# The sample group's slots in the attention of a hybrid decoder step: key products earlier, value products further apart, two cache buffers exchanged

## The reference

```python
DIL_CONFIGS = ((128, 1), (512, 4), (2048, 16))
kc = jnp.concatenate([win_k, k], axis=1)      # sample group: cached rows, then the new ones
vc = jnp.concatenate([win_v, v], axis=1)
for _, dil in DIL_CONFIGS:
    o_i, l_i = dilated_branch_sample(q, kc, vc, dil)
...
attn = combine_branches(outs, lses).reshape(B, T, ATTN_WIDTH)
```

## Time and profile before

| what | value |
|---|---|
| median of 3 runs | 1748.76 us (1748.57 to 1753.09) |
| profiled execution | 1746.06 us, span 1744.3 us |
| TensorE matmul busy | 1688.0 us, 97% |
| VectorE, ScalarE busy | 1112.6 us (64%), 914.3 us (52%) |
| stage of the change | about 345 to 524 us |

### The profile page before, as it was taken

The page is one execution under the profiler, slowest core; times in us unless marked ns, Lnnn a source line. Parts: engine busy times, 40 slices in busy tenths (PEclk is TensorE's granted clock), DMA queues, the critical chain, the costliest instruction groups (busy, mean ns, idle before and its releaser), DMA issues.

```text
span 1744.3 us, 29781 instructions
## 1 busy us (share of the span) xinstructions
PE 1688.0 (97%) x11750; PEld 1576.6 (90%) x11750; DVE 1112.6 (64%) x2055; ACT 914.3 (52%) x1673; POOL 2.2 (0%) x12
## 2 busy tenths in 40 slices
PE   7999999989999999999998999999999999999998
PEld 7999999845669999888778999999999999999998
DVE  5489998777665776435457767644676534676533
ACT  7534434755666675545455555444545433555433
POOL 0000000000000000000000000000000000000000
PEclk9999999999999999999999999999999999999999
DMA  9899967495215645443533444444445444445443
GB/s 284 197 248 217 239 169 164 157 323 223 86 56 166 187 139 164 146 133 110 177 95 104 122 121 137 138 133 142 135 138 157 139 136 144 135 134 154 139 138 100
DMA packets 400672, 271.44 MB, mean 156 GB/s; under 512 B 54251, under 2 KB 374881, under 8 KB 399183
## 3 DMA queue, kind: packets, MB, share of 16 engines
q1 hardware_dynamic: 395688, 260.72, 51.9%
q10 hardware_dynamic: 4847, 8.83, 1.5%
HBM read 225.40 MB, written 27.23 MB: 145 GB/s over the span
## 4 chain that ended last, share of the span: by engine, by line
PE 79%; DVE 7%; ACT 5%; DMA 4%; issue 3%; SPq 1%; ACTq 1%; DVEq 0%
PE bank L1344 74%; PE bank L1341 5%; DMA raw<-in_w_in_dram 1%; ACT whi L702 1%; ACT WORDS L823 1%; DVE C L1957 1%; DMA raw<-in_w_mv_dram 1%; DVE wlo L1970 1%; ACT wide L716 1%; DVE cv L1957 1%; DVE Pp L1961 1%; DMA cached<-in_cache_win_v_dram 0%; DVE Y L1957 0%; DMA cached_t<-keys_turned 0%; DVE RSCF L2093 0%
## 5 line engine op out<-in xcount | busy, mean ns | idle before, releaser
L1344 PE MATMUL bank<-op_hi,whi 128*128 128x352 f32 x1632 | 538.8, 330 | 5.1 <-DVE wlo L1970 2.9
L1970 DVE TENSOR_TENSOR wlo<-raw,whi 128x1024 fp32r<-128x1024 f32 (+1 forms) x312 | 374.3, 1201 | 261.0 <-ACT whi L702 260.4
L1344 PE MATMUL bank<-op_hi,wlo 128*128 128x352 f32 x1632 | 524.6, 321 | 0.0
L1344 PE MATMUL bank<-op_lo,whi 128*128 128x352 f32 x1632 | 523.8, 321 | 0.0
L702 ACT ACTIVATE whi<-raw 128x1024 fp32r<-128x1024 f32 (+1 forms) x312 | 325.2, 1043 | 318.8 <-DMA raw<-in_w_down_dram 95.6
L1344 PEld LDWEIGHTS bank<-op_hi,whi 128*128 128x128 f32 x1632 | 306.9, 188 | 14.8 <-issue 10.1
L1344 PEld LDWEIGHTS bank<-op_lo,whi 128*128 128x128 f32 x1632 | 307.9, 189 | 0.6
L1344 PEld LDWEIGHTS bank<-op_hi,wlo 128*128 128x128 f32 x1632 | 306.6, 188 | 0.0
L1344 PE MATMUL bank<-fhi,whi 128*128 128x352 f32 x528 | 171.2, 324 | 0.0
L1344 PE MATMUL bank<-fhi,wlo 128*128 128x352 f32 x528 | 170.7, 323 | 0.0
L1344 PE MATMUL bank<-h1hi,whi 128*128 128x352 f32 x480 | 159.9, 333 | 3.4 <-DVE wlo L1970 3.4
(11 more groups left out here) (290 smaller groups left out, 2274.7 us busy)
## 6 DMA issues: line engine op xcount, KB each, us to landing
raw<-in_w_up_dram SPq DMA_DIRECT2D x132, 512.0 KB, 3.8
raw<-in_w_down_dram SPq DMA_DIRECT2D x48, 512.0 KB, 4.1
raw<-in_w_out_dram SPq DMA_DIRECT2D x24, 512.0 KB, 4.3
raw<-in_w_xq_dram SPq DMA_DIRECT2D x24, 512.0 KB, 4.2
raw<-in_w_xo_dram SPq DMA_DIRECT2D x24, 512.0 KB, 4.2
PLANES<-HALVES SPq DMA_DIRECT2D x96, 112.0 KB, 3.7
keys_turned<-WORDS SPq DMA_DIRECT2D x24, 448.0 KB, 3.2
cached_t<-keys_turned SPq DMA_DIRECT2D x6, 1792.0 KB, 9.5
```

The costliest lines, as they stand in the source:

```text
L1344: return pe.matmul(out, lhsT, rhs, start=first, stop=last, skip_group_check=shared)
L1970: dve.tensor_tensor(wlo[v % SLOTS][:, 0:nk, :], raw[v % SLOTS][:, 0:nk, :], whi[v % SLOTS][:, 0:nk, :].bitcast(F32), ALU.subtract).then_in ...
```

## The change

`PLACES` exchanges the first two buffers: `cached[0]` now lies at 160064, and `cached[1]` at 47104. The queue loads window 0 (k0) at the place where it loaded window 1, and window 1 (k1) after `LAST_IN`, where it loaded window 0. The order of all other windows stays.

The slots are now written out by hand. Group 0: key products at 3, 8, 13 and 17, masked maximum 19, exponential 20, scaling 22, turning Ps 23, PTS 24, value products 25, 30, 34 and 38, copy 40, turn and small copies 41. Group 1: batches 4 and 5 at 3 and 7, tiles at 8 to 21, masked maximum 23, exponential 24, scaling 26, turning Ps 27, PTS 28, value products 29, 33, 36 and 39, copy 41, turn 42. `product_bank` follows the tiles: in the steps that hold tiles the product for the prompt uses bank 3.

```diff
--- before.py
+++ after.py
@@ -209,7 +209,7 @@
     stage_f = mn("stage_f", 146656, [P, 3, P])
 
 
-    PLACES = (47104, 160064, 119808)
+    PLACES = (160064, 47104, 119808)
     cached = [mn(f"cached{i}", o, [P, KTILES, AW]) for i, o in enumerate(PLACES)]
     cached_t = [mn(f"cached_t{i}", o, [P, AT, KEYS]) for i, o in enumerate(PLACES)]
     HALVES = [mn(f"HALVES{i}", 160064 + 3584 * i, [P, 2, KEYS], U16) for i in range(2)]
@@ -339,8 +339,11 @@
     STEPS = [(i, hp) for i in range(TT) for hp in range(AT)]
     NP = len(STEPS)
     LAST_P2 = max(s for s in range(NP) if s % 3 == 2)
-    GROUP = 4 * KTILES
     SAMPLE = 44
+    KEYS_DONE = (18, 22)
+    BATCH_AT = {(0, 3): 0, (0, 8): 1, (0, 13): 2, (0, 17): 3, (1, 3): 4, (1, 7): 5}
+    VALUE_AT = {(0, 25): 0, (0, 30): 1, (0, 34): 2, (0, 38): 3, (1, 29): 4, (1, 33): 5, (1, 36): 6, (1, 39): 7}
+    GATHERED_AT = (40, 41)
     ORDER_W = [(kind, b) for g in range(2) for kind in "kv" for b in range(4 * g, 4 * g + 4)]
     EARLY = 14
     EARLY_OUT = 4
@@ -376,7 +379,8 @@
         return n % 3 != 0
 
     def key_tile(g, r):
-        return g * GROUP + r if 0 <= r < GROUP and (g * GROUP + r) // KTILES >= AHEAD else -1
+        n = 8 * KTILES - KEYS_DONE[1] + r
+        return n if g == 1 and FIRST_TURNED <= n < 8 * KTILES else -1
 
     def product_bank(s):
         return 3 if any(key_tile(*sample_slot(s + 3, pos)) >= 0 for pos in range(3)) else 4
@@ -386,10 +390,6 @@
 
     def pieces_until(u):
         return sum(n for v, n in PIECES_AT.items() if v < u)
-
-    def batch_slot(r):
-
-        return r // KTILES if 0 <= r < GROUP and r % KTILES == KTILES - 1 else -1
 
     QTS = [[(0, P), (P, P), (2 * P, (CW if c < CH - 1 else SP0) - 2 * P)] for c in range(CH)]
     SLOT = {("mix", 2): 0, ("mix", 0): 1, ("mix", 1): 0, ("xq", 2): 1, ("xq", 0): 0, ("xq", 1): 1,
@@ -566,7 +566,7 @@
                     sp.wait_ge(*at(f"kept{i}", PIECES - 2 + i))
                 load(wt[:, :], A["prompt_bias"], "tables", "p")
                 load(ws[:, :], A["sample_bias"], "tables", "s")
-                window(1)
+                window(0)
             weight(u)
             if u in GATHER_AT:
                 gather_old(GATHER_AT[u])
@@ -584,7 +584,7 @@
                     load(stage_u[:, i, :], A["state_conv"].rearrange("a b t c -> (a b t) c")[i * 120:(i + 1) * 120, :], "states", ("u", i))
 
         sp.wait_ge(*at("unit", LAST_IN))
-        window(0)
+        window(1)
         sp.wait_ge(*at("csq_used", 2 * CH - 1))
         sp.wait_ge(*at("cn", (CONV_ORDER[CH - 1], CT - 1)))
         window(2)
@@ -903,16 +903,16 @@
                 if n >= FIRST_TURNED + 2:
                     act.wait_ge(*at("ssc", ("tile", n - 2)))
                 act.activation(KTS[n % 2][:, :, :], bank[4 + n % 2][:, :].rearrange("p (k n) -> p k n", k=AT), ACT.Copy).then_inc(*mark("ktsa", n))
-            if r == GROUP + 2:
+            if r == KEYS_DONE[g] + 2:
                 act.wait_ge(*at("smax", g))
                 act.activation(Ps[:, :], Ps[:, :], ACT.Exp, bias=negm[:, 2:3], accum_out=den[:, 2:3]).then_inc(*mark("sexp", g))
-            if r == GROUP + 6:
+            if r == KEYS_DONE[g] + 6:
                 act.wait_ge(*at("sptr", g))
                 if g:
                     act.wait_ge(*at("spv", 3))
                 act.activation(PTS[:, 4:7, :], bank[7][:, 0:384].rearrange("p (a n) -> p a n", n=P), ACT.Copy).then_inc(*mark("spta", (g, 0)))
                 act.activation(PTS[0:NS, KTILES, :], bank[7][0:NS, 384:512], ACT.Copy).then_inc(*mark("spta", (g, 1)))
-            if r == GROUP + 14:
+            if r == GATHERED_AT[g]:
                 act.wait_ge(*at("spv", 4 * g + 3))
                 if g:
                     act.wait_ge(*at("sot", 0))
@@ -1600,13 +1600,13 @@
                 group_scores(g)
             if key_tile(g, r - 1) >= 0:
                 key_scores(key_tile(g, r - 1))
-            elif batch_slot(r) >= 0:
-                batch_scores(4 * g + batch_slot(r))
-            if r == GROUP + 5:
+            elif (g, r) in BATCH_AT:
+                batch_scores(BATCH_AT[g, r])
+            if r == KEYS_DONE[g] + 5:
                 turn_ps(g)
-            if r - GROUP - 7 in (0, 2, 4, 6):
-                window_product(4 * g + (r - GROUP - 7) // 2)
-            if r == GROUP + 15:
+            if (g, r) in VALUE_AT:
+                window_product(VALUE_AT[g, r])
+            if r == GATHERED_AT[g] + 1:
                 take(5, "satt", (g, 3, 1))
                 pe.wait_ge(*at("os", g))
                 for b in range(4):
@@ -2185,8 +2185,8 @@
                 if n >= FIRST_TURNED + 2:
                     dve.wait_ge(*at("ssc", ("tile", n - 2)))
                 dve.tensor_copy(KTS[n % 2][:, :, :], bank[4 + n % 2][:, :].rearrange("p (k n) -> p k n", k=AT)).then_inc(*mark("ktsd", n))
-            if r == GROUP + 1:
-                dve.wait_ge(*at("ssc", 3 if g == 0 else ("tile", 2 * GROUP - 1)))
+            if r == KEYS_DONE[g] + 1:
+                dve.wait_ge(*at("ssc", 3 if g == 0 else ("tile", 8 * KTILES - 1)))
                 if g:
                     dve.wait_ge(*at("sptr", g - 1))
                 pieces_s = ((0, 512, bank[6][:, 0:512], ws[:, 0:512]), (512, KEYS, bank[7][:, 0:KEYS - 512], ws[:, 512:KEYS]),
@@ -2197,17 +2197,17 @@
                     masked_max(Ps[:, k0:k1], src, bias, mx[:, 0, k:k + 1], mx[:, 0, k - 1:k] if k else -3e38).then_inc(*mark("sm", (g, k)))
                 dve.wait_ge(*at("sm", (g, 2)))
                 dve.tensor_scalar(negm[:, 2:3], mx[:, 0, 2:3], -1.0, None, ALU.mult).then_inc(*mark("smax", g))
-            if r == GROUP + 4:
+            if r == KEYS_DONE[g] + 4:
                 dve.wait_ge(*at("sexp", g))
                 dve.reciprocal(rden[:, 2:3], den[:, 2:3]).then_inc(*mark("srd", g))
                 dve.wait_ge(*at("srd", g))
                 dve.tensor_scalar(Ps[:, :], Ps[:, :], rden[:, 2:3], None, ALU.mult).then_inc(*mark("spn", g))
-            if r == GROUP + 6:
+            if r == KEYS_DONE[g] + 6:
                 dve.wait_ge(*at("sptr", g))
                 if g:
                     dve.wait_ge(*at("spv", 3))
                 dve.tensor_copy(PTS[:, 0:4, :], bank[6][:, :].rearrange("p (a n) -> p a n", n=P)).then_inc(*mark("spt", g))
-            if r == GROUP + 15:
+            if r == GATHERED_AT[g] + 1:
                 dve.wait_ge(*at("sot", g))
                 for b in range(4):
                     v = bank[5][:, b * P:(b + 1) * P].rearrange("p (k y) -> p k y", y=32)
```

## The result

The changed kernel took 1756.14 us (median of nine runs, 1750.58 to 1758.99), the kernel before 1748.89 us on the same chip (nine runs, 1743.3 to 1753.09). The ratio, estimated from the runs, is 1.0033 [1.0021, 1.0045] (the brackets are its 95% interval; the quotient of the medians alone would be 1.0041): **slower by 0.33%, some 5.8 us**. That is at the edge of what the prediction called measurable. The sign of the sum was right (+1.8), its size was three times too small: applied to the median that the prediction started from, the ratio gives 1748.76 x 1.0033 = 1754.5 us, at the upper end of its range (1744.5 to 1755); the median as measured, 1756.14, lies 1.1 above that end.

The account below looks back on a forecast made before the run. TensorE, busy 97% of the span, was taken as the bound, with VectorE bounding steps 4 to 11. Terms +2.0 - 2.0 - 0.4 = -0.4, plus 2.2 for the clock, gave +1.8 us: 1750.5 us, range 1744.5 to 1755.

Parts of the forecast that it names:

- Buffers: nothing: Exchanging the places of k0 and k1: the 0.45 us wait for k0 goes, nothing else changes in the queue there.
- Group 0: +2.0 and +2.2 for the clock: Up to step 15: 2.0 us lost without the clock, 2.2 more from a fall to 1.2 GHz behind the gap before Ps.
- TensorE waits 0.9: Step 5, fourth key product: reached at 363.6, k3's load lands at 364.5, so TensorE waits 0.9 us.
- the chain crossing three small steps: Reason given for group 0's 2.0 us loss: the softmax chain crosses three small steps where TensorE has little else to do.
- a good place for them is in steps 4 to 10: Group 0: VectorE bounds steps 4 to 11, so key products are well placed in steps 4 to 10; no size of its own.
- Steps 15 to 19: gain 2.0: Group 1: gaps of 3.4 us behind VectorE get filled with six more tiles, one 1.4 us gap stays; gain 2.0 us.
- Group 1 behind them: gain 0.4: Second masked maximum holds scores 24 by 1.6 us, Ps waits 0.6, product 0.1, against 1.7, 0.5 and 0.5 before; gain 0.4.
- Later steps are TensorE's own limit, and work moved among them is worth nothing: Group 1 behind step 19: TensorE itself sets the pace, so moving work among these steps gains nothing.
- Rival 1: Gap before Ps: the clock does not fall because VectorE is faster than counted; -0.4 us, 1748.4 us; chance 0.27.
- Rival 2: Attention: the waits go and the chain is hidden, all 7.5 us come back, 1741.3 us; chance of over 5.2 us 0.08.
- Rival 3: Group 0: low clock holds until the fourth value product; slower by more than 0.3%, 1757 us; chance 0.12.
- Rival 4: Step 5: k3 lands later still because v0's load runs beside it; +2.5 us more, 1753 us; chance 0.08.

Follow-up runs that it names:

- e1: Changed kernel with all slots of both groups put back, only the buffers changed: 1748.59 us, ratio 0.999 to the kernel before.
- e2: Changed kernel with group 1's slots put back, so only group 0 and the buffers changed: 1756.00 us, ratio 1.0033 to the kernel before.
- e4: Changed kernel with the load of v0 issued only when k3 has landed: 1757.56 us, ratio 1.0038 to the kernel before.
- e5: Changed kernel with turning Ps, PTS copies and each group's first value product one slot later: 1753.83 us, ratio 1.0036 to the kernel before.
- e9: Against e1, only group 0's key products moved to slots 3, 8, 13 and 17: 1755.66 us, ratio 1.0025 to the kernel before.
- e10: Changed kernel with seven extra unused matmuls filling the gap before group 0's turns of Ps: 1756.50 us, ratio 1.0035 to the kernel before.
- e12: Kernel of e7 with group 0's key products at slots 6, 11, 16 and 20: 1747.99 us, ratio 0.9997 to the kernel before.
- e3: Changed kernel with group 0's slots put back, so only group 1 and the buffers changed: 1752.95 us, ratio 1.0008 to the kernel before.
- e6: e3 with group 1's value products back at their old slots: 1750.26 us, ratio 1.0005 to the kernel before.
- e7: e6 with group 1's tiles, masked maximum, softmax and turn of Ps one slot later: 1747.29 us, ratio 0.9988 to the kernel before.
- e8: Changed kernel with group 0's fourth key product and softmax chain three slots later, value products at 28, 32, 35, 38: 1754.62 us, ratio 1.0033 to before.

## Why the prediction was right and wrong

**Buffers: nothing.** Right (e1); k0's product waited for nothing.

**Group 0: +2.0 and +2.2 for the clock.** The mechanism was right: the gap before Ps was forecast at 4.2 us and was 4.46, the clock fell behind it and stayed low for about 6.8 us (twice what 0.53 and 0.79 lack of 1.00, times 5 us) against 6.5, and no value window was late. In e2's trace the low stretch was longer, 10.2 us by the same count (0.86, 0.50 and 0.62 in the windows of 365 to 380). Step 15 was forecast 60.1 us after the first scores, clock included; it came at 61.88 here and at 60.27 in e2. That e2 is so near is luck: its k3 was early by 1.4 us and its low clock long. The miss of 1.8 us in the changed kernel is the term "TensorE waits 0.9" for k3. Its load landed 0.5 us later than forecast, counted from the first scores (19.7 against 19.2), and TensorE reached the product 1.3 us sooner (16.9 against 18.3), so the wait was 0.9 + 0.5 + 1.3 = 2.7. The 0.5 is k2's: k3 landed 5.8 us after k2, close to the 5.9 of the prediction (in the trace of before it is 6.1), and k2 landed 0.5 later than forecast, after 9.5 us instead of 9.0. The early arrival costs nothing, the late landing does, and the longer wait brought a clock fall of its own, which made the product 1.27 us slower: 0.5 + 1.3. e4 shows the second of the two missing when the product runs at full clock. Five other traces have the same key slots; k3 landed at 17.8 in three of them (e2, e5, e9) and at 19.5 to 19.6 in two (e10, e4). This term needed a range, not a value.

I had put group 0's loss down to the chain crossing three small steps. e9 adds what I missed: moved forward, the key products cost 3.8 us in its trace and, by the ratios, some 6 us against e1, even when the chain stays. 1.4 us are lost by step 8, where VectorE now waits for scores behind key products. That is at odds with the prediction's own sentence that a good place for them is in steps 4 to 10, since two of them went to steps 1 and 2. The rest comes in steps 8 to 11, which they had filled: TensorE waits longer there and, in both traces (e9, e12), the clock falls.

**Steps 15 to 19: gain 2.0.** Right, 2.1.

**Group 1 behind them: gain 0.4.** Here the prediction failed, by 5.8 us in the traces. The parts that it named were there in their sizes (scores 24 held by 1.6, measured 1.62; Ps 0.6, measured 0.60), and the step that failed is the sentence "Later steps are TensorE's own limit, and work moved among them is worth nothing". Value products in the last steps filled holes; moved forward they left the holes open, and the attention became 3.0 us longer (e3 to e6). And the wait of 1.6 was balanced against waits of before that were as long, without asking what the clock does: before, the windows of 465 to 480 us, with the waits of group 1 in them, had the clock at 1.00; behind the new wait it was lower in six of the seven traces that have it. Wait and clock together cost 2.4 us (e6 to e7, in which the tiles move a slot as well). 3.0 and 2.4 are the 5.4 lost behind step 20.

**The number.** The range held by luck. Its upper end was the price of a clock that doubles all work behind the gap of group 0; in the traces what filled it was group 1, for which the range had no term, and the late k3. By the times group 0 alone already has the whole 0.33% (e2), 5.8 us against a forecast of 4.2.

**Rivals.** Rival 1 (no clock fall) did not happen; the gap was as counted. Rival 2 (all waits vanish) did not either: they moved to other operations. Rival 3 had the right side but the wrong reason: the low stretch ended after about 6.8 us, well short of the 13 from which it decides (10.2 in e2). The Trainium skill (TensorE: Matmul & The Clock Gate, "Part 4: PE-mode transpose") would have had the turns of steps 7 to 10 not count; in the windows of 380 to 385 the clock came back with turns and short scores in the mix, though products ran among them, so the run neither proves nor refutes the rule for turns alone. The Trainium skill's section "HAM oscillation — how this bites in real kernels" on the same page makes the gaps the cost. The gap before Ps agrees: in all four traces with 4.45 to 5.03 us there (changed, e2, e4, e8) the clock fell. The shorter waits went either way: behind 2.46 us for k3 (e10) the product was slow, behind 2.48 (e4) it was not. Rival 4 came near the size (k3's wait 1.8 us longer, 2.5 in the rival), and e4 shows the cause to be another.

**What stays open.** What makes k3 land at 17.8 or at 19.6 us. It mostly follows k2: where k2 landed at 12.5 to 12.7 (e2, e5, e9), k3 came at 17.8, where k2 landed at 13.7 to 14.0 (changed, e4, e8), at 19.6, though in these three k3 was issued 0.9 to 2.3 us earlier; but in e10 k2 came at 12.8 and k3 at 19.5. What decides whether the clock falls behind a wait of 1.6 to 2.5 us. Whether turning Ps later (e5) gains anything. And the pair of traces says 9.3 us for the attention, the ratio 5.8 for the whole (3.7 to 7.9 by its interval). One pair of traces does not give the typical loss: e2's, with the same group 0, reaches step 15 1.6 us sooner, and behind step 15 traces with the changed slots differ by up to 1.1 us (e8, e3) and with the old ones by 2.3 (e2, e9).

## What to carry to other kernels

Work that is spread among steps is a filler, so before moving it count what the steps it leaves will wait for, not only what it meets where it goes; a late stretch that looks full of TensorE work can still have holes that only more work shows. Where another engine sets the pace, don't put work ahead of what that engine waits for. Where an operation waits at the head of an in-order queue, ask what stands behind it that the engine it waits for could use. Price each new wait with the clock fall that may follow it, as a chance and not as a certainty, and give a load that lands within a microsecond or two of its use a range. Before reading a difference of a microsecond or two from one pair of traces, look how far traces with the same code in that stretch differ.

## What was not expected of the hardware

The same wait in the same place was followed by the lower clock in one trace and not in another. The 1.62 us before scores 24 stand in seven traces; behind them the clock was lower in six (in the 5 us windows, 0.76 in the changed kernel and 0.66 in e3, e6, e8 and e10; 0.80 and 0.86 in e4) and at 1.00 in e5. The 1.86 before step 11, with group 0's old slots, stand in six traces; the clock fell in e3 alone (0.79 and 0.87). The 1.69 before the second Ps stand in four; it fell in e9 alone (0.66). A wait's length did not decide it, and neither did the code.

The third of three loads of 1.8 MB in a row took 8.1 to 13.0 us in these traces, the second 7.3 to 9.9; holding back the load behind it (e4: 9.6 and 11.6) changed neither. Seven matmuls of 128x512 in float32, recorded as 14, took 6.17 us at full clock, 0.44 for each record.
